# A two-block model in fp32: grouped columns at the start, gates woven into the convolution, the first expert without spreads, and the output ahead of the branches

## What is computed

```python
def first_block(...):                                   # two layers
    for l in range(DEPTH):
        shift, scale, gate = jnp.split(c_act @ w_ada[l] + b_ada[l], 3, axis=-1)
        h = rmsnorm(x, norm_g[l]) * (1.0 + scale[:, None, :]) + shift[:, None, :]
        mq, mk, mv, mo, mz, mi, mf, rq, rk, rv, rz = split_cols(h @ w_in[l])
        # four mLSTM heads: conv and silu of mq, mk; input and forget gates mi, mf (one column a head each)
        # four retention heads: rotary of rq, rk; fixed decay
        x = x + gate[:, None, :] * (jnp.concatenate([y_m, y_r], axis=-1) @ w_out[l])
    return rmsnorm(x, final_g)
def moe_swiglu(h, ...):                                 # last part of the second block, 8 experts, 2 a token
    logits = t @ w_router + b_router
    top_w = jax.nn.softmax(top_val, axis=-1)
    for e in range(N_EXPERTS):
        out = out + combine[:, e:e + 1] * swiglu(t, w_gate[e], w_up[e], w_down[e])
```

## Time and profile before

| what | value |
|---|---|
| time before, median of 3 runs | 2194.29 us (2193.09 to 2195.05) |
| the profiled execution | 2192.89 us, its span 2191.1 us |
| TensorE, weight loads, VectorE, ScalarE busy | 97%, 85%, 81%, 61% |
| mean granted clock of TensorE | 0.993 |
| read from HBM | 593.89 MB, 273 GB/s over the span |

### The profile page before, as it was taken

One profiled execution on the slowest core, in us unless ns is written; L12 is line 12 of the kernel. 1 busy time (PEld: TensorE's weight loads), 2 busy tenths in 40 slices (PEclk: granted clock), 3 DMA queues, 4 the chain that ended last, 5 costly groups with the idle time before them and its releaser, 6 DMA issues.

```text
span 2191.1 us, 33917 instructions
## 1 busy us (share of the span) xinstructions
PE 2135.8 (97%) x13601; PEld 1870.0 (85%) x13601; DVE 1769.4 (81%) x2172; ACT 1342.0 (61%) x1287; POOL 32.3 (1%) x61
## 2 busy tenths in 40 slices
PE   6999999999999999999999999999999999999998
PEld 3899999899998889999977888888888888888886
DVE  4988875877766878887878888888888888888887
ACT  2655555565645753434756676776777766776675
POOL 3000000000000000000000000000000000000000
PEclk9999999999999999999999999999999999999999
DMA  9677854666656548987446999999999999999995
GB/s 296 212 233 231 251 185 149 213 195 204 200 176 212 174 140 286 305 306 263 145 176 222 335 352 339 366 347 343 349 342 373 338 341 346 359 355 341 349 342 213
DMA packets 357219, 597.17 MB, mean 273 GB/s; under 512 B 10409, under 2 KB 201401, under 8 KB 357065
## 3 DMA queue, kind: packets, MB, share of 16 engines
q1 hardware_dynamic: 353920, 589.02, 77.7%
q0 software_dynamic: 2752, 5.86, 1.2%
q10 hardware_dynamic: 392, 0.13, 0.0%
HBM read 593.89 MB, written 4.22 MB: 273 GB/s over the span
## 4 chain that ended last, share of the span: by engine, by line
PE 87%; DVE 6%; ACT 3%; issue 2%; DMA 2%; SPq 0%; DVEq 0%; ACTq 0%
PE ps L1575 9%; PE ps L1577 9%; PE ps L1576 9%; PE ps L1097 6%; PE ps L1098 6%; PE ps L1099 6%; PE ps L1605 5%; PE ps L1604 5%; PE ps L1603 5%; PE ps L1122 3%; PE ps L1123 3%; PE ps L1124 3%; PE ps L1108 2%; PE ps L1550 2%; PE ps L1109 1%
## 5 line engine op out<-in xcount | busy, mean ns | idle before, releaser
L1658 DVE TENSOR_TENSOR wlo<-raw,whi 128x2048 fp32r<-128x2048 f32 x487 | 1114.1, 2289 | 278.8 <-ACT whi L692 259.0
L692 ACT CAST whi<-raw 128x2048 fp32r<-128x2048 f32 x487 | 929.4, 1909 | 414.8 <-PE ps L1577 144.9
L1097 PE MATMUL ps<-hhi,whi 128*128 128x256 f32 x1424 | 410.3, 288 | 2.6 <-DVE wlo L1658 2.4
L1098 PE MATMUL ps<-hlo,whi 128*128 128x256 f32 x1424 | 402.6, 283 | 0.0
L1099 PE MATMUL ps<-hhi,wlo 128*128 128x256 f32 x1424 | 402.5, 283 | 0.0
L1575 PE MATMUL ps<-whi,xghi 128*128 128x512 f32 x896 | 364.8, 407 | 0.7 <-DVE wlo L1658 0.7
L1577 PE MATMUL ps<-wlo,xghi 128*128 128x512 f32 x896 | 353.9, 395 | 0.0
L1576 PE MATMUL ps<-whi,xglo 128*128 128x512 f32 x896 | 353.8, 395 | 0.0
L1097 PEld LDWEIGHTS ps<-hhi,whi 128*128 128x128 f32 x1424 | 272.5, 191 | 10.3 <-issue 7.0
L1098 PEld LDWEIGHTS ps<-hlo,whi 128*128 128x128 f32 x1424 | 272.7, 191 | 0.3
L1099 PEld LDWEIGHTS ps<-hhi,wlo 128*128 128x128 f32 x1424 | 272.6, 191 | 0.0
(11 more groups left out here) (388 smaller groups left out, 3026.6 us busy)
## 6 DMA issues: line engine op xcount, KB each, us to landing
raw<-in_moe_w_gate_dram SPq DMA_DIRECT2D x114, 1024.0 KB, 5.2
raw<-in_moe_w_up_dram SPq DMA_DIRECT2D x112, 1024.0 KB, 5.2
raw<-in_moe_w_down_dram SPq DMA_DIRECT2D x112, 1024.0 KB, 4.9
raw<-in_w_in_dram SPq DMA_DIRECT2D x92, 1024.0 KB, 5.2
raw<-in_w_ada_dram SPq DMA_DIRECT2D x69, 1024.0 KB, 7.8
raw<-in_w_out_dram SPq DMA_DIRECT2D x24, 1024.0 KB, 4.9
raw<-in_ffn_w_gate_dram SPq DMA_DIRECT2D x11, 1024.0 KB, 9.0
raw<-in_ffn_w_up_dram SPq DMA_DIRECT2D x11, 1024.0 KB, 8.1
```

Source lines behind the costliest of these rows:

```text
L692: nc.scalar.copy(whi[:, u.hl, :], raw[:, u.raw, :]).then_inc(hi_ready, 1)
L1097: mm(ps2[u.bank][:, j], whi[:, u.hl, w], hhi[:, k], start=k == 0, stop=False)
L1098: mm(ps2[u.bank][:, j], whi[:, u.hl, w], hlo[:, k], start=False, stop=False)
L1658: V.tensor_tensor(wlo[:, u.hl, :], raw[:, u.raw, :], whi[:, u.hl, :].bitcast(F32), ALU.subtract).then_inc(raw_free, 1)
```

## The change

Five parts, in the order of the run. (1) Start: TensorE takes all eight row blocks of each w_ada unit, block k into the 32 output rows of group k % 4, with the conditioning column as the first of 32, the others zero (`cfirst`). VectorE has no part in it. ScalarE copies all 128 rows, and the turning products add the groups up. Norms 0 and 1 write `hhi` at once. (2) The gate weights are split in hi and lo (`ghi`, `glo`, forget gates in the second group of 32 columns), and the gate sums become 24 products with `hhi` and `hlo`. GpSimd's queue waits for six w_ada units before its first load. (3) In the first head of a layer VectorE waits for the gate sums ahead of the convolution, puts the scans between its second and third tap, makes one head's diagonals, and the other three later; the w_ada unit of step 1 goes behind the split of z; the angles go behind the split of rk. In layer 0 the w_ada units take other places (1, 2, 4 ... 14, 15). (4) The router's products go into groups; the count of tokens per expert gets a signal of its own; GpSimd's clearing of `pickT` and `moe` goes. (5) The first expert has no spreads, the second copies instead of adding, the last adds `moe` to xT during its down units. The last result's spreads and the output's transposition and copies stand ahead of the branch; in the branch they would be done again. Loads, copies and splits beyond the eighth expert go.

```diff
-N_FULL = (0, 1, 6)
+N_FULL = (6,)
...
     if l == 0:
-        return j // 2 if j >= 0 and j % 2 == 0 else None
+        return {1: 0, 15: 8}.get(j, j // 2 if 0 < j < 16 and j % 2 == 0 else None)
...
-                    if l == 0 and j == 2:
+                    if l == 0 and j == 4:
                         sp.dma_start(cst[:, P:C_BEFORE], consts[:, P:C_BEFORE]).then_inc(const_in, 16)
...
-            pool.dma_start(posi[:], positions[0:1, :].broadcast_to([P, S])).then_inc(pos_in, 16)
+            pool.wait_ge(ada_done, ADA_START - 2)
             for l in range(L):
...
-            pool.wait_ge(htok_done, 4)
-            nc.gpsimd.memset(pickT[:], 0.0).then_inc(pickT_ready, 1)
-            nc.gpsimd.memset(moe[:], 0.0).then_inc(moe_cleared, 1)
+            nc.gpsimd.memset(rb[:], 0.0).then_inc(rb_clear, 1)
+            pool.wait_ge(rb_clear, 1)
+            pool.dma_start(rb[0:NE], b_router[0].rearrange("(e o) -> e o", o=1)).then_inc(router_in, 16)
...
+            def gates_high(l):
+                act.wait_ge(gate_in, 16 * 3 * L)
+                for i in range(2):
+                    nc.scalar.copy(ghi[:, :, GROUP * i:GROUP * i + H], wgate[:, l, :, H * i:H * i + H]).then_inc(ghi_ready, 1)
...
-                    for k in range(ADA_SPLIT, KD):
-                        mm(o, cact[:, 0, k:k + 1], w[:, 256 * k:256 * k + 256], start=k == ADA_SPLIT, stop=False)
-                    pe.wait_ge(ada_free, a.sums())
-                    last = mm(o, ones[:, 0:1], acc[:, a.n % HALF], start=False, stop=True)
+                for k in range(KD):
+                    g = GROUP * (k % 4)
+                    last = mm(ps[ADA_START_BANK[a.n // 2]][g:g + GROUP, S * (a.n % 2):S * (a.n % 2) + S], cfirst[:, k],
+                              w[:, S * k:S * k + S], start=k < 4, stop=k >= 4, skip_group_check=True)
...
-                        for g in range(2):
-                            for d in range(KD):
-                                last = mm(ps2[6][0:H, g], wgate[:, l, d, g * H:(g + 1) * H], h[:, d], start=d == 0, stop=d == KD - 1)
+                        for d in range(KD):
+                            mm(sums, ghi[:, d], hhi[:, d], start=d == 0, stop=False)
+                            mm(sums, ghi[:, d], hlo[:, d], start=False, stop=False)
+                            last = mm(sums, glo[:, d], hhi[:, d], start=False, stop=d == KD - 1)
...
-                last = mm(ps[7][0:NE, 0:S], wr[:, k], h[:, k], start=k == 0, stop=k == KD - 1)
+                g = GROUP * (k % 4)
+                last = mm(ps[7][g:g + NE, 0:S], wr[:, k], h[:, k], start=k < 4, stop=k >= 4, skip_group_check=True)
...
-                    if i % 4 == 3 and 1 <= c <= 4:
+                    if i % 4 == 3 and 1 <= c <= 4 and 1 <= job.n < NE:
...
+            spread_all(Job(NE))
+            turn_output(4 * (norm_no(N_FFN[1]) + 1))
             pe.wait_ge(jobs_ready, 1)
             nx = pe.value_load(jobs[0:1, 0:1], min_val=0, max_val=3)
             with pe.If(nx > 0):
...
                     low(k.plus(LOOK))
-                    ada_after(1)
-                    if hd.n == 0:
-                        angles()
+                    if h_no == 0:
+                        gates_taken(l)
+                    else:
+                        ada_after(1)
                     dve.wait_ge(taken_s, hd.count(7, 2))
                     for tap in range(CONV_K):
+                        if h_no == 0 and tap == 2:
+                            gates_summed(l)
...
                     if h_no == 0:
-                        gates(l)
+                        gates_spread(l, [0])
+                        gates_columns(l)
                     low(v.plus(LOOK))
+                    if h_no == 0:
+                        ada_after(1)
                     ada_after(2)
                     if h_no:
                         retention_finish(hd.before)
                     low(o.plus(LOOK))
                     ada_after(3)
+                    if h_no == 0:
+                        gates_spread(l, range(1, H))
...
                     low(z.plus(LOOK))
+                    if hd.n == 0:
+                        angles()
```

More of the change, by code:

```diff
@@ L1059, in _, with take_output @@
             for g in range(NE // 2):
-                expert(Job(0, g, 2), Gather(3, g), Gather(1, g))
-                expert(Job(1, g, 2), Gather(1, g), None)
+                expert(Job(2 * g), Gather(3, g), Gather(1, g))
+                expert(Job(2 * g + 1), Gather(1, g), None)
+            def take_output(times):
+                for half in range(2):
+                    act.wait_ge(out_turned, 2 * times + half + 1)
+                    nc.scalar.copy(otok[:, 0, 512 * half:512 * half + 512], ps[4 + half][:, :]).then_inc(first_ready, 1)
+            take_result(Job(NE))
+            take_output(0)
             act.wait_ge(jobs_ready, 1)
@@ L1067, in _ @@
                         take_tokens(Gather(2, j), half)
+                    for i in range(LOOK):
+                        high(Job(NE, j).unit(i))
                     expert(Job(NE, j), Gather(2, j), None)
-            take_result(Job(NE, nx))
-            for half in range(2):
-                act.wait_ge(out_turned, half + 1)
-                nc.scalar.copy(otok[:, 0, 512 * half:512 * half + 512], ps[4 + half][:, :]).then_inc(first_ready, 1)
+                    take_result(Job(NE + 1, j))
+                take_output(1)
         @block.tensor
@@ L2329, in _, with add_last, take_output @@
             for g in range(NE // 2):
-                expert(Job(0, g, 2), Gather(1, g))
-                expert(Job(1, g, 2), None)
+                expert(Job(2 * g), Gather(1, g))
+                expert(Job(2 * g + 1), None)
+            def add_last(job, done):
+                for p in range(4):
+                    dve.wait_ge(spread_done, job.count(4, p - 3))
+                    for d in (2 * p, 2 * p + 1):
+                        last = V.scalar_tensor_tensor(xT[:, d], ps2[p][:, d % 2], mod[:, gate + d:gate + d + 1], xT[:, d], ALU.mult, ALU.add)
+                    last.then_inc(done, 1)
+            def take_output(times):
+                for half in range(2):
+                    dve.wait_ge(out_turned, 2 * times + half + 1)
+                    V.tensor_copy(otok[:, 1, 512 * half:512 * half + 512], ps[6 + half][:, :]).then_inc(second_ready, 1)
+            dve.wait_ge(moe_added, KD)
+            add_last(Job(NE), x_ready)
+            take_output(0)
             dve.wait_ge(jobs_ready, 1)
@@ L2341, in _ @@
                         take_tokens(mine, half)
+                    for i in range(LOOK):
+                        low(Job(NE, j).unit(i))
                     expert(Job(NE, j), None)
[L2343 to L2357 removed]
+                    dve.wait_ge(x_ready, 4 * (norm_no(N_FFN[1]) + 2))
+                    add_last(Job(NE + 1, j), spread_taken)
+                take_output(1)
 def _shape_constants():
```

303 lines of the change are left out of this document (143 added, 160 removed).

## The result

The changed kernel takes 2178.0 us (median of 4 runs, 2177.91 to 2181.92), beside 2194.4 for the kernel before (4 runs, 2193.09 to 2195.05): a ratio of 0.9931, 95% interval 0.9917 to 0.9945. The forecast was 2170.5, range 2161 to 2181. The profiled run took 2177.91 us with a span of 2176.1, so 15.0 us of the span are gone, where the sum had 23.8.

What follows compares the result with a forecast made beforehand. TensorE, busy for 97% of the span, was taken as the bound, so only less matrix work or closed gaps win time. The terms summed to -23.8 us from 2192.89, giving 2169.1, and 2170.5 as median; range 2161 to 2181.

Steps and rivals of the forecast that it cites:

- Start, -15.9: Start of layer 0: bound by w_ada transfers, the q product starts at 39.1 instead of 55.03 us; bounds -12 and -18.
- Head 0 of layer 0, +4.0: Gate sums to values: VectorE ends last, 32.6 instead of 28.6 us, although 4.2 us of matrix work went.
- its +0.8: Head 0 of each layer: low clock behind a gap of some 4 us costs 0.8 us a layer.
- Norm of layer 1, -1.4: Norm of layer 1: loses the full h, but the split of k stands behind it; -1.4 us, bounds 0 and -2.8.
- Head 0 of layer 1, -0.4 and +0.8 for the clock: Gate sums to values in layer 1: 27.6 instead of 28.0 us, plus 0.8 for the low clock behind a gap.
- Router, -3.0: Router: grouped products -0.7, two counting products behind the signal -0.9, GpSimd's clearing gone -1.4; bounds -1.5 and -3.5.
- First expert, -3.5: First expert: four rounds of spreads at 0.86 us go; -3.5 us, bounds -3 and -3.6.
- End, -5.2: End: spreads follow the first half copy, the copy ends at 2182.3 instead of 2187.53 us; -4 if the branch ends last.
- the untaken branch passes beside it: End: the untaken branch, some 3 us from the last transpose, passes beside the store's last 3.6 us.
- Given back: Rival: first-expert load stands, low clock for longer, late adjacent ada units in heads 1 and 3; 5 to 10 us, 2178; chance 0.12.
- The slower rival: Rival: gate weights through GpSimd's queue land late while VectorE works; break-even 75 us, at 85 the kernel takes 2204; chance 0.04.
- the weave that hides itself: Rival: VectorE isn't the bound in head 0, both layers keep 4.2 us, the norm 2.8; 2155.5 us; chance 0.08.

## Why the prediction was right or wrong

- **Start, -15.9: right in the cause, 1.8 too much.** TensorE waits for the transfers, as named. The last ada unit landed at 35.84, 0.7 earlier than the 36.5 that I had read from the backlog, and TensorE began it at 36.55 only because the turning ahead of it was slow; that this agrees with 36.5 is luck. The term that was mis-sized is TensorE's work: I took 0.9 and 1.0 us, at the full clock of rows 5, though I had just made TensorE wait for transfers. It measured 1.93 and 1.87; filled with products it was 1.07 and 1.12, and the q product came at 39.2, against 39.1 forecast. The 3.2 us of GpSimd's packets measured 2.7.
- **Head 0 of layer 0, +4.0: right, to the tenth** (28.6 to 32.6), and by the chain that was named. The runs show what is in it: the ada unit costs 3.5 us in this stretch, the angles 1.6 (in a kernel with other edits too), and the weave gives 2.9. The clock was at 0.50 behind the stand, but its +0.8 wasn't seen as a cost of its own, since VectorE ended last.
- **Heads 1 to 3: no term for them, and that is the first step that failed.** I had two units in a row only in a rival. It cost 2.8 us: 0.7 in head 1, 1.3 in head 2, 0.7 in head 3; with one of the two places mended 1.5 came back.
- **Norm of layer 1, -1.4: -0.8**, within its bounds.
- **Head 0 of layer 1, -0.4 and +0.8 for the clock: +2.8.** The stand came as forecast (3.91 us), the clock term was mis-sized. From the stand on TensorE did at 0.50 what it was to do at 1.00: 0.98, 2.07 and 2.93 us for unit, broadcast and scores, and the front of the z product. I had priced a fall of the clock by the q product behind the norm, which VectorE's tiles pace anyway; here nothing else paced it. Without the stand the stretch is 24.8 us.
- **Router, -3.0: -2.0**, inside its bounds. VectorE's pair takes 0.36 us instead of 1.76, and the counting products gained as said. The products in groups gave nothing: they follow ScalarE's h one by one, at the low clock, in 3.05 us, and end 1.1 us behind the last h, where the old ones ended 1.0 behind it. And 0.6 us went into the slower turning of the logits, which the sum didn't have.
- **First expert, -3.5: -3.7.**
- **End, -5.2: -2.5.** The branch's gap closed as said; up to the last copy it is -4.5, the spreads starting 0.77 behind the product's end and taking 3.69. The step that failed is "the untaken branch passes beside it". It does pass, but packets of instructions run beside the stores, and the last store lands at 4.3 us instead of 2.7 (2.7 again without the branches). I had allowed for a branch that ends last, not for one that slows the transfer.
- **Rivals.** "Given back", with 2178, is what happened: 8.8 us of the forecast went, to two ada units in a row and to the clock, two of its three causes, and at the end, which it didn't name. I had given it 0.12 and the forecast 0.67. The slower rival and the weave that hides itself didn't come true.
- **The number.** 2178.0 lies in the range of 2161 to 2181, but 7.5 above the forecast and on the number of a rival: the sign and the large terms were right, the point wasn't. And the range's upper end doesn't follow from its two named parts, 3.9 for the start and half of the 7.5 given back, which make 2178.2; by those the measured time would have been only just inside.

## What to carry to other kernels

When matrix work is cut until the engine waits for transfers, price what follows the wait at the low clock, unless another engine paces it; and when an engine in a chain waits for a result, give it the piece of work that depends on nothing (here one ada unit, 4.8 us) ahead of that wait. Before tuning the order of work, shift the operands of the longest products by 32 bytes and measure: one unused tile of that size was worth as much as this whole change (16.7 us beside the kernel with 64 bytes, against 16.4), though it made other products slower. A branch behind the last copies, while the stores run, costs 1.7 us in the traces here.

## What was new about the hardware

- **The place of an operand within 64 bytes.** With 128x128 stationary operands in fp32r at a multiple of 64 bytes a product of 512 columns takes 0.227 to 0.228 us from start to start (987.7 us of experts), 32 bytes past one 0.233 (1008.5); the places are counted from the first tile. A shift of 64 bytes leaves the experts at 1007.9. It isn't a rule that a multiple of 64 is faster: in products of 256 columns with stationary weights at a multiple of 64, a moving operand at a multiple of 64 goes with 0.120 us, one 32 bytes past it with 0.117 to 0.118. So in the layers, where both are at a multiple of 64, it is 0.120 in every kernel. Why isn't shown. The kernel before had the slow place in its experts too.
- **The clock behind a stand.** It was 0.50 behind stands of 3.5, 3.8, 3.9 and 8.3 us, and stayed there well into the work that followed: from 28 to 44 us in the start, from 397 to 401 in layer 1, from 84 to 92 behind the 8.3. Moving a stand can thus cost more than the stand. Products that nobody reads kept it at 1.00 in the start where two waits of 0.6 and 0.7 us were left; where five of 0.4 to 1.3 us were left, it fell to 0.50 at the q product all the same. They gained 1.5 us in the start and nothing at the norms; in the gather no gain is shown, since one kernel without them was as fast (3.81 us).
- **A branch while the last stores run.** With it the DMA queues hold four packets of instructions beside the stores, and the last store lands 4.3 us after its issue; without it there are none, and it lands after 2.7. That it is these packets which hold the store up is inferred.
